# Feature-wise matrix products: three matmuls of 256 columns into the same PSUM columns in place of one of 512 and one of 256 with an addition

## The chip, the core and the metric

The kernel is one program on one core of a Trainium2 chip. The metric is the time of one execution on the device, in microseconds (us). The kernel before was timed in three runs: 2785.09, 2785.18 and 2785.83 us, median 2785.18. One more execution was recorded by the profiler; the rows below come from that one.

## The reference, cut to what matters

The program computes two transformer blocks on 256 tokens of width 2048, in float32. The first block is a sliding-window attention and a gated feed-forward network (`D_FF` 5632). The second is a hybrid mixer (gated linear attention and a pooled branch), a cross-attention to a memory of 256 tokens, and a feed-forward network with a short convolution. Most of the work is products of a normalised activation with a weight matrix:

```python
def swiglu(h, w_gate, w_up, w_down):
    return (silu(h @ w_gate) * (h @ w_up)) @ w_down

def conv_glu_ffn(h, w_up, conv_w, conv_b, w_down):
    u = h @ w_up
    u = conv(u) + conv_b            # along the tokens, one filter for each feature
    gate, val = u[..., :D_FF_2], u[..., D_FF_2:]
    return (silu(gate) * val) @ w_down

q = (h @ w_cq); k = mem_n @ w_ckv[:, :2048]    # cross-attention, queries and keys
```

## The kernel before, in words

**Units.** The function `weight_units` (lines 55 to 99) lists 920 units. A unit is one slice of a weight matrix, 256 rows by 512 columns (512 KB). All engines go through the units in this order, each with its own program. SyncE loads the slice into one of five buffers `raw` (line 376). ScalarE rounds it to float32r, `whi` (line 857), VectorE takes the remainder, `wlo = raw - whi` (line 1273); both have four buffers. The activations lie in SBUF transposed and split in the same way, as `XA`, `XB` or `XC`: `X[w.x][:, k, 0, :]` is the high part of 128 features by 256 tokens and `X[w.x][:, k, 1, :]` the low part. A product of two split numbers is made of three terms, high by high, low by high and high by low; low by low is left out.

**Two kinds of units.** In a row-wise unit (`rows_unit`, lines 426 to 436) the activation is the stationary operand (the weights of the array, 128 columns) and the weight slice is the moving one: lines 433, 434 and 435, 512 columns each, 12 matmuls in a unit. In a feature-wise unit (`feature_unit`, lines 438 to 447) the weight slice is stationary and the activation moves, so the output has the features in the partitions. The change is there. It serves the first projections of both feed-forward networks (`ffn`, lines 67 to 72, 16 feature-wise units for each 512 features), the queries and keys of the linear attention (lines 80 and 81) and of the cross-attention (lines 91 to 94). That is 432 of the 920 units, and 8 pairs of matmuls in each. Line 445 multiplies the high weights with high and low activations side by side, 512 columns, so a PSUM bank holds high-by-high in columns 0 to 255 and high-by-low in columns 256 to 511. Line 446 adds low-by-high, 256 columns, to the first half. Each matmul has a weight load of its own.

**Eviction.** Eight feature-wise units sum up four banks of 128 features each. Then ScalarE copies the second half of a bank to SBUF (`tile_copy` line 968, `qk_copy` line 1037, `cross_copy` line 1107), one bank in each of the next four units. VectorE adds the first half to the copy (`tile_sum` line 1477, `qk_sum` line 1553, `cross_sum` line 1665) and multiplies the sum with a broadcast row of the inverse norms (lines 1482, 1557, 1671). The rest of a feed-forward tile (convolution, silu, product, split into `XB`) follows in later units.

**What sets the order.** Each engine's program is written out by hand as a loop over `u`, with tables (`TILES`, `QK`, `CQK` and others) that say at which `u` a piece of side work stands. TensorE waits before a unit for its split weights (`s.lo`, line 842), for its activation (`operand`) and, at the first unit of a bank group, for the banks' readers (`banks_clear`, lines 712 to 795): for a feature-wise bank on `s.fsum`, `s.gs` or `s.cs`, raised by the addition. ScalarE and VectorE split the weights three units ahead of TensorE (`split_until`, line 345).

Of the kernel before, what the change touches and what calls it, by code (L numbers as in the profile page):

```python
# [11 lines left out]
ACT = mybir.ActivationFunctionType  # L12
AX = mybir.AxisListType

P = 128
# [86 lines left out]
UNITS = weight_units()  # L102
# [73 lines left out]
class Region:  # L176
# [21 lines left out]
    act dve ones xtr xhi xlo sq rms rrt rs dg wd wide res  # L198
    table sine rope mask kv ksq kms krt krope ktr kT
    qe qsq qms qrt qrs qrope qtr qT sco mx exp pn ptr pT pv bxh bx  # L200
    fc fsum fu fw fv silu fm hh hx fzero
    wah wal gn am aT gz lt ln ls pe pm pc pw pxh px cum bT
    gqc gs gqk ge gexp gx gp gsel gB gv sr go gsq gms grt og ogt ogh ogx sg m1 mg mT mxh mx2
    cc cs ckq csc cmx cexp cpn cpt cpT vm cpv oxh ox
    fsq fy fms frt frs yd ya"""


# [3 lines left out]
def build(nc, d):  # L211
# [75 lines left out]
    gX = B.take("gX", [P, 4, 256])  # L287
    gA = B.take("gA", [P, 2, 4, P])
    gB = B.take("gB", [P, 4, P])
    gt = B.take("gt", [P, 4, 256])  # L290
    M.new()
    gv = M.take("gv", [P, 2, 1024])
    sr = M.take("sr", [P, 2, 1024])
# [21 lines left out]
    vm = M.take("vm", [P, 2, D])  # L315
    cp = [M.take(f"cp{i}", [P, 2, 256]) for i in range(2)]
    cpT = [M.take(f"cpT{i}", [P, 2, 256]) for i in range(2)]
    ct = M.take("ct", [P, 4, 256])
    csm = M.take("csm", [P, 32])

    space["A"].new()
# [95 lines left out]
    def tensor():  # L417
# [20 lines left out]
        def feature_unit(u, w):  # L438
            i = u % NSPL
            for j in range(2):  # L440
                both = X[w.x][:, w.xk + j, :, :]
                high = X[w.x][:, w.xk + j, 0, :]
                for f in range(4):
                    b, c = w.banks[f], slice(f * P, (f + 1) * P)
                    pe.matmul(ps[:, b, :], whi[:, i, j, c], both, start=w.begin and j == 0, stop=False)  # L445
                    end = pe.matmul(ps[:, b, 0:256], wlo[:, i, j, c], high, start=False, stop=w.end and j == 1)  # L446
            end.then_inc(s.unit, 1)

        def feed(n, c, bank):
# [199 lines left out]
        def cross_scores(h):  # L649
            pe.wait_ge(s.ckq, 4 * (4 + h) + 4)  # L650
            if h == 0:
                pe.wait_ge(s.cs, 28)
            else:
                pe.wait_ge(s.cexp, h)
            for t in range(2):
                for j in range(4):
                    e = pe.matmul(ps[:, 2, t * 256:(t + 1) * 256], qcT[:, 4 * h + j, t * P:(t + 1) * P],  # L657
                                  kmT[:, 4 * h + j, :], start=j == 0, stop=j == 3)
            e.then_inc(s.csc, 1)
# [7 lines left out]
        def cross_values(h):  # L667
            pe.wait_ge(s.vm, h + 1)
            pe.wait_ge(s.cpT, h + 1)
            if h == 0:  # L670
                pe.wait_ge(s.cs, 32)
            else:
                pe.wait_ge(s.ox, 2 * h)
            for j in range(4):
                for m in range(2):
                    e = pe.matmul(ps[:, j // 2, (j % 2) * 256:(j % 2) * 256 + 256],  # L676
                                  vm[:, m, h * 512 + j * P:h * 512 + (j + 1) * P], cpT[h % 2][:, m, :],
                                  start=m == 0, stop=m == 1)
                if j % 2 == 1:
                    e.then_inc(s.cpv, 1)  # L680
# [31 lines left out]
        def banks_clear(u, w):  # L712
# [13 lines left out]
                    pe.wait_ge(s.res, 2)  # L726
            elif w.weight in ("ffn_w_down", "w_down_2"):
                e, ch = u // U_F2, (w.k // 16) * 4 + (2 if w.k >= 32 else 3)
                pe.wait_ge(s.fsum, tile(e, ch, w.acc // 2, 1 + 2 * (w.acc % 2)) + 1)
            elif U_F1 <= u < U_IN or U_F2 <= u:  # L730
                e = u // U_F2
                base = (U_F1, U_F2)[e]
# [2 lines left out]
                if ch == 0 and which == 0:  # L735
                    pe.wait_ge(s.res, 3 if e == 0 else 23)
                    pe.wait_ge(s.xlo, 2 * FEED_AT[(1, 5)[e], 2] + 2)
                elif ch == 0:
                    pe.wait_ge(s.res, 4 if e == 0 else 24)
                    pe.wait_ge(s.xlo, 2 * FEED_AT[(1, 5)[e], 3] + 2)  # L740
                    pe.wait_ge(s.wide, 1 if e == 0 else 5)
                elif ch % 4 == 0:
                    pe.wait_ge(s.res, (0, 20)[e] + ch + 2 + 2 * which)
                else:
                    pe.wait_ge(s.fsum, tile(e, ch - 1, which, 3) + 1)
            elif u == U_IN:
                pe.wait_ge(s.res, 15)
            elif u == U_IN + 8:
# [4 lines left out]
                pe.wait_ge(s.pe, 2)  # L753
                pe.wait_ge(s.bT, 2)
            elif u in (U_IN + 32, U_IN + 40):
                pe.wait_ge(s.gs, 2 if u == U_IN + 32 else 6)
            elif u in (U_IN + 48, U_IN + 56):
                pe.wait_ge(s.gv, 1 if u == U_IN + 48 else 2)
            elif U_IN + 64 <= u < U_OUT:
# [14 lines left out]
            elif U_CK <= u < U_CV:  # L774
                j = (u - U_CK) // 8
                if j < 2:
                    pe.wait_ge(s.res, 19 + j)
                    pe.wait_ge(s.xlo, 2 * FEED_AT[4, 2 + j] + 2)
                    if j:
                        pe.wait_ge(s.wide, 4)  # L780
                else:
                    pe.wait_ge(s.cs, 4 * (j - 1))
            elif U_CV <= u < U_CO:
                n = (u - U_CV) // 8
                if n < 2:
                    pe.wait_ge(s.cs, 26 + 4 * n)
                else:
                    pe.wait_ge(s.vm, n - 1)
            elif w.weight == "w_co_2":
                if w.acc < 2:  # L790
                    pe.wait_ge(s.vm, 3 + w.acc)
                elif w.acc == 2:
                    pe.wait_ge(s.cpT, 4)
                else:
                    pe.wait_ge(s.ox, 8)
# [54 lines left out]
    def scalar():  # L850
# [110 lines left out]

        def tile_copy(u, e, ch, which, f):
            w = UNITS[u - 1 - f]
            if f == 0:
                act.wait_ge(s.unit, u)
            act.activation(ft[e][which][:, f, :], ps[:, w.banks[f], 256:512], ACT.Copy).then_inc(s.fc, 1)

        def tile_conv(e, ch, which, f):  # L970
            n = which * NF + ch * 4 + f
            act.wait_ge(s.fu, tile(e, ch, which, f) + 1)
# [57 lines left out]
                act.wait_ge(s.cum, b + 1)  # L1030
                act.copy(bT[:, 2 * b:2 * b + 2, :], ps[:, 2 + b, :].rearrange("p (h t) -> p h t", t=256)).then_inc(s.bT, 1)

        def qk_copy(u, i):
            f = i % 4
            if f == 0:
                act.wait_ge(s.unit, u)
            act.activation(gt[:, f, :], ps[:, UNITS[u - 1 - f].banks[f], 256:512], ACT.Copy,
                           scale=1.0 if i >= 4 else float(128 ** -0.5)).then_inc(s.gqc, 1)

        def level_exp(n):  # L1040
            act.wait_ge(s.ge, n)
            act.activation(gE[:, :, :], gE[:, :, :], ACT.Exp).then_inc(s.gexp, 1)
# [56 lines left out]
                e.then_inc(s.mxh, 1)  # L1099

        def cross_copy(u, i):
            f = i % 4
            if f == 0:
                act.wait_ge(s.unit, u)
            act.activation(ct[:, f, :], ps[:, UNITS[u - 1 - f].banks[f], 256:512], ACT.Copy).then_inc(s.cc, 1)

        def cross_exp(h):
            scale = 512 ** -0.5  # L1110
# [47 lines left out]
        for u in range(U_END + 1):  # L1158
# [33 lines left out]
                query_root(q_root_at[u])  # L1192
            if u in ATTEND:
                exponents(ATTEND[u])
            if u in TILES:
                tile_copy(u, *TILES[u])
            if u in tiles1:
                e, ch, which, f = tiles1[u]
                if e == 1:
# [22 lines left out]
                pool_map(POOL2[u])  # L1222
            if u == MI + 22:
                decays()
            if u in QK:
                qk_copy(u, QK[u])
            if u in level_exp_at and level_exp_at[u] < 8:
                level_exp(level_exp_at[u] + 1)
            if u == MI + 55:
# [16 lines left out]
            if u in CQK:  # L1246
                cross_copy(u, CQK[u])
            if u in CSC:
                cross_exp(CSC[u])
            if u in c_turn_at:  # L1250
# [16 lines left out]
    def vector():  # L1267
# [204 lines left out]

        def tile_sum(u, e, ch, which, f):
            n = tile(e, ch, which, f)
            t, off = ft[e][which][:, f, :], 2 * e
            dve.wait_ge(s.fc, n + 1)
            dve.scalar_tensor_tensor(out=t, in0=ps[:, UNITS[u - 1 - f].banks[f], 0:256], scalar=1.0, in1=t,
                                     op0=ALU.mult, op1=ALU.add).then_inc(s.fsum, 1)
            dve.wait_ge(s.fsum, n + 1)
            if f == 0 and ch == 0:  # L1480
                dve.wait_ge(s.wide, (1, 5)[e])
            dve.tensor_tensor(fu[e][which][:, f, off:off + 256], t, wideX[:, :], ALU.mult).then_inc(s.fu, 1)

        def tile_conv(e, ch, which, f):
            n, t = tile(0, ch, which, f), ft[e][which][:, f, :]
# [63 lines left out]

        def qk_sum(u, i):  # L1550
            f = i % 4
            dve.wait_ge(s.gqc, i + 1)
            dve.scalar_tensor_tensor(out=gt[:, f, :], in0=ps[:, UNITS[u - 1 - f].banks[f], 0:256],
                                     scalar=1.0 if i >= 4 else float(128 ** -0.5), in1=gt[:, f, :],
                                     op0=ALU.mult, op1=ALU.add).then_inc(s.gs, 1)
            dve.wait_ge(s.gs, i + 1)
            dve.tensor_tensor((gk if i >= 4 else gq)[:, f, :], gt[:, f, :], wideX[:, :], ALU.mult).then_inc(s.gqk, 1)

        def level_select(n):
            L = STEPS[n]  # L1560
# [100 lines left out]

        def cross_sum(u, i):
            f, n = i % 4, i // 4 % 4
            dve.wait_ge(s.cc, i + 1)
            dve.scalar_tensor_tensor(out=ct[:, f, :], in0=ps[:, UNITS[u - 1 - f].banks[f], 0:256], scalar=1.0,
                                     in1=ct[:, f, :], op0=ALU.mult, op1=ALU.add).then_inc(s.cs, 1)
            dve.wait_ge(s.cs, i + 1)
# [3 lines left out]
            dve.tensor_tensor(o[:, 4 * n + f, :], ct[:, f, :], wide[:, :], ALU.mult).then_inc(s.ckq, 1)  # L1671

        def cross_max(h):
            mx = csm[:, h * 4:h * 4 + 2]
# [212 lines left out]
```

## Time and profile before

| | |
|---|---|
| Median of three runs | 2785.18 us |
| The profiled execution, its own time | 2785.57 us |
| Its span, first to last instruction | 2784.3 us |
| TensorE matmuls, busy | 2734.6 us, 98% |
| TensorE weight loads, busy (under the matmuls) | 2297.5 us, 83% |
| VectorE busy | 1686.0 us, 61% |
| ScalarE busy | 1372.0 us, 49% |
| DMA | 495.5 MB, mean 178 GB/s |
| Mean granted TensorE clock | 0.993 of full speed |

Busy time is the union of the times in which an engine had at least one instruction in flight. Matmuls are pipelined: a matmul begins before the one in front of it has left the array, so the listed duration of one is longer than the time for which it holds the engine. How often they start tells that. Idle time is listed with what ended it.

### The profile page before, as it was taken

How to read it: one execution, taken by the hardware profiler on the slowest of the kernel's cores; microseconds unless marked ns; L12 is line 12 of the kernel's file. 1: busy time of each engine (PE TensorE's matmuls, PEld its weight loads, DVE VectorE, ACT ScalarE, POOL GpSimd, SP SyncE). 2: the span in 40 equal slices, each digit the busy share in tenths (PEclk: the TensorE clock that was granted, in tenths of full speed). 3: DMA queues.
4: the chain of work that ended last, by engine and by line, in shares of the span. 5: the costliest groups of instructions: out<-in, count | busy, mean ns of one | idle time of the engine just before them, and what ended most of it. 6: DMA issues, size and time to landing. Idle time of an engine off the chain costs nothing.

```text
span 2784.3 us, 34701 instructions
## 1 busy us (share of the span) xinstructions
PE 2734.6 (98%) x13940; PEld 2297.5 (83%) x13940; DVE 1686.0 (61%) x2438; ACT 1372.0 (49%) x2040; POOL 0.2 (0%) x4
## 2 busy tenths in 40 slices
PE   8989999999999998999999999999999999999998
PEld 7667888888888886888888888888888888888886
DVE  6666566556655664474555655544568756775676
ACT  6665544444434454445444544444455544553554
POOL 0000000000000000000000000000000000000000
PEclk9999999999999999999999999999999999999999
DMA  6324666666666666768696555554566566656654
GB/s 224 114 91 129 183 186 189 191 188 184 186 197 182 189 179 163 161 157 173 190 190 195 203 183 182 188 161 143 181 181 198 188 198 178 195 179 204 183 188 144
DMA packets 256994, 495.54 MB, mean 178 GB/s; under 512 B 17201, under 2 KB 18481, under 8 KB 256322
## 3 DMA queue, kind: packets, MB, share of 16 engines
q1 hardware_dynamic: 256834, 493.33, 60.1%
q8 instruction: 110, 1.80, 0.3%
q14 instruction: 50, 0.41, 0.0%
HBM read 491.17 MB, written 2.10 MB: 177 GB/s over the span
## 4 chain that ended last, share of the span: by engine, by line
PE 95%; ACT 2%; DVE 2%; DMA 1%; SPq 0%; issue 0%; ACTq 0%; DVEq 0%
PE ps L445 29%; PE ps L433 15%; PE ps L435 15%; PE ps L434 15%; PE ps L446 15%; PE ps L423 1%; PE ps L512 1%; ACT whi L857 1%; PE ps L615 1%; PE ps L676 1%; PE ps L532 1%; PE ps L657 0%; DMA raw<-in_w_in 0%; ACT sS L946 0%; DVE sS L1459 0%
## 5 line engine op out<-in xcount | busy, mean ns | idle before, releaser
L857 ACT CAST whi<-raw 128x1024 fp32r<-128x1024 f32 x920 | 965.4, 1050 | 1259.3 <-PE ps L435 635.1
L1273 DVE TENSOR_TENSOR wlo<-raw,whi 128x1024 fp32r<-128x1024 f32 x920 | 1121.5, 1221 | 689.8 <-ACT whi L857 688.6
L445 PE MATMUL ps<-XA,whi 128*128 128x512 f32 x1792 | 633.4, 399 | 0.0
L445 PE MATMUL ps<-XC,whi 128*128 128x512 f32 x1664 | 588.4, 399 | 0.0
L446 PE MATMUL ps<-XA,wlo 128*128 128x256 f32 x1792 | 502.9, 281 | 0.0
L446 PE MATMUL ps<-XC,wlo 128*128 128x256 f32 x1664 | 467.3, 281 | 0.0
L445 PEld LDWEIGHTS ps<-XA,whi 128*128 128x128 f32 x1792 | 336.7, 188 | 83.4
L433 PE MATMUL ps<-whi,XB 128*128 128x512 f32 x960 | 377.3, 393 | 0.0
L445 PEld LDWEIGHTS ps<-XC,whi 128*128 128x128 f32 x1664 | 312.7, 188 | 77.7
L435 PE MATMUL ps<-whi,XB 128*128 128x512 f32 x960 | 374.3, 390 | 0.0
L434 PE MATMUL ps<-wlo,XB 128*128 128x512 f32 x960 | 374.2, 390 | 0.0
L446 PEld LDWEIGHTS ps<-XA,wlo 128*128 128x128 f32 x1792 | 338.4, 189 | 0.2
L446 PEld LDWEIGHTS ps<-XC,wlo 128*128 128x128 f32 x1664 | 314.3, 189 | 0.2
L433 PE MATMUL ps<-whi,XA 128*128 128x512 f32 x736 | 294.2, 400 | 0.9 <-DVE wlo L1273 0.9
L435 PE MATMUL ps<-whi,XA 128*128 128x512 f32 x736 | 288.5, 392 | 0.0
L434 PE MATMUL ps<-wlo,XA 128*128 128x512 f32 x736 | 288.4, 392 | 0.0
L433 PEld LDWEIGHTS ps<-whi,XB 128*128 128x128 f32 x960 | 180.6, 188 | 39.4 <-issue 2.5
L435 PEld LDWEIGHTS ps<-whi,XB 128*128 128x128 f32 x960 | 180.5, 188 | 37.8
L434 PEld LDWEIGHTS ps<-wlo,XB 128*128 128x128 f32 x960 | 180.7, 188 | 36.5
L433 PEld LDWEIGHTS ps<-whi,XA 128*128 128x128 f32 x736 | 139.4, 189 | 33.6 <-issue 5.3
L435 PEld LDWEIGHTS ps<-whi,XA 128*128 128x128 f32 x736 | 139.3, 189 | 30.0
L434 PEld LDWEIGHTS ps<-wlo,XA 128*128 128x128 f32 x736 | 139.5, 190 | 27.7
(225 smaller groups left out, 1899.1 us busy)
## 6 DMA issues: line engine op xcount, KB each, us to landing
raw<-in_w_up SPq DMA_DIRECT2D x176, 512.0 KB, 3.8
raw<-in_w_in SPq DMA_DIRECT2D x128, 512.0 KB, 5.1
raw<-in_ffn_w_gate SPq DMA_DIRECT2D x88, 512.0 KB, 3.8
raw<-in_ffn_w_up SPq DMA_DIRECT2D x88, 512.0 KB, 3.8
raw<-in_ffn_w_down SPq DMA_DIRECT2D x88, 512.0 KB, 3.7
raw<-in_w_down SPq DMA_DIRECT2D x88, 512.0 KB, 3.7
raw<-in_w_ckv SPq DMA_DIRECT2D x64, 512.0 KB, 4.1
raw<-in_attn_w_qkv SPq DMA_DIRECT2D x40, 512.0 KB, 4.0
```

The lines of the kernel that those rows point to most:

```text
L423: t = pe.transpose(ps[:, bank, c0 + i * P:c0 + (i + 1) * P], src, ident)
L433: pe.matmul(o, xh, whi[:, i, j, :], start=w.begin and j == 0, stop=False)
L434: pe.matmul(o, xh, wlo[:, i, j, :], start=False, stop=False)
L435: end = pe.matmul(o, xl, whi[:, i, j, :], start=False, stop=w.end and j == 1)
L445: pe.matmul(ps[:, b, :], whi[:, i, j, c], both, start=w.begin and j == 0, stop=False)
L446: end = pe.matmul(ps[:, b, 0:256], wlo[:, i, j, c], high, start=False, stop=w.end and j == 1)
L512: e = pe.matmul(ps[:, b, m * nk:(m + 1) * nk], qT[c % 2][:, h, qb * P:(qb + 1) * P], kT[:, c, 0:nk], start=False, stop=m == len(heads) - 1)
L532: e = pe.matmul(ps[64 * (h % 2):64 * (h % 2) + 64, 7, (m // 2) * P:(m // 2 + 1) * P], vt[:, kb, c * 64:c * 64 + 64], pT[n % NPT][:, (m * ( ...
L615: e = pe.matmul(o, left[:, h, t * P:(t + 1) * P], r, start=True, stop=True)
L676: e = pe.matmul(ps[:, j // 2, (j % 2) * 256:(j % 2) * 256 + 256], vm[:, m, h * 512 + j * P:h * 512 + (j + 1) * P], cpT[h % 2][:, m, :], st ...
L857: act.copy(whi[:, u % NSPL, :, :], raw[:, u % NRAW, :, :]).then_inc(s.hi, 1)
L1273: dve.tensor_tensor(wlo[:, u % NSPL, :, :], raw[:, u % NRAW, :, :], whi[:, u % NSPL, :, :].bitcast(F), ALU.subtract).then_inc(s.lo, 1)
```

## The change

A feature-wise product is now three matmuls of 256 columns into columns 0 to 255 of its bank: high weights by high activations, high weights by low activations, low weights by high activations. The second half of the bank is not used. The copies on ScalarE and the additions on VectorE are gone with their buffers `gt` and `ct`; the product with the broadcast row reads PSUM directly (for the linear attention's queries and keys, with the scale in the same instruction). VectorE waits for the unit itself (`s.unit`) at the first of four tiles. TensorE's waits for cleared banks go to the semaphores of those products (`s.fu`, `s.gqk`, `s.ckq`) with the same counts. The diff shows the feed-forward tiles; the linear attention's and the cross-attention's copies, sums and waits change in the same way.

```diff
@@ feature_unit
             for j in range(2):
-                both = X[w.x][:, w.xk + j, :, :]
-                high = X[w.x][:, w.xk + j, 0, :]
+                high, low = X[w.x][:, w.xk + j, 0, :], X[w.x][:, w.xk + j, 1, :]
                 for f in range(4):
-                    b, c = w.banks[f], slice(f * P, (f + 1) * P)
-                    pe.matmul(ps[:, b, :], whi[:, i, j, c], both, start=w.begin and j == 0, stop=False)
-                    end = pe.matmul(ps[:, b, 0:256], wlo[:, i, j, c], high, start=False, stop=w.end and j == 1)
+                    o, c = ps[:, w.banks[f], 0:256], slice(f * P, (f + 1) * P)
+                    pe.matmul(o, whi[:, i, j, c], high, start=w.begin and j == 0, stop=False)
+                    pe.matmul(o, whi[:, i, j, c], low, start=False, stop=False)
+                    end = pe.matmul(o, wlo[:, i, j, c], high, start=False, stop=w.end and j == 1)
             end.then_inc(s.unit, 1)
@@ banks_clear
-                pe.wait_ge(s.fsum, tile(e, ch, w.acc // 2, 1 + 2 * (w.acc % 2)) + 1)
+                pe.wait_ge(s.fu, tile(e, ch, w.acc // 2, 1 + 2 * (w.acc % 2)) + 1)
...
-                    pe.wait_ge(s.fsum, tile(e, ch - 1, which, 3) + 1)
+                    pe.wait_ge(s.fu, tile(e, ch - 1, which, 3) + 1)
@@ scalar
-        def tile_copy(u, e, ch, which, f):
-            w = UNITS[u - 1 - f]
-            if f == 0:
-                act.wait_ge(s.unit, u)
-            act.activation(ft[e][which][:, f, :], ps[:, w.banks[f], 256:512], ACT.Copy).then_inc(s.fc, 1)
@@ vector
         def tile_sum(u, e, ch, which, f):
             n = tile(e, ch, which, f)
-            t, off = ft[e][which][:, f, :], 2 * e
-            dve.wait_ge(s.fc, n + 1)
-            dve.scalar_tensor_tensor(out=t, in0=ps[:, UNITS[u - 1 - f].banks[f], 0:256], scalar=1.0, in1=t,
-                                     op0=ALU.mult, op1=ALU.add).then_inc(s.fsum, 1)
-            dve.wait_ge(s.fsum, n + 1)
-            if f == 0 and ch == 0:
+            off = 2 * e
+            if f == 0:
+                dve.wait_ge(s.unit, u)
                 dve.wait_ge(s.wide, (1, 5)[e])
-            dve.tensor_tensor(fu[e][which][:, f, off:off + 256], t, wideX[:, :], ALU.mult).then_inc(s.fu, 1)
+            dve.tensor_tensor(fu[e][which][:, f, off:off + 256], ps[:, UNITS[u - 1 - f].banks[f], 0:256], wideX[:, :],
+                              ALU.mult).then_inc(s.fu, 1)
```

## Rows read from the trace of the kernel before

**Rows 1.** The page, busy us (share of the span) and instructions of each engine.

```profile
PE 2734.6 (98%) x13940; PEld 2297.5 (83%) x13940; DVE 1686.0 (61%) x2438; ACT 1372.0 (49%) x2040; POOL 0.2 (0%) x4
```

**Rows 2.** Waits of TensorE's matmuls, longest first: total us, times, longest.

```profile
PE ps L532 <- DVE XB L1467: 15.1, 10, 4.1
PE ps L544 <- DVE wal L1514: 9.9, 1, 9.9
...
PE ps L676 <- ACT vm L1125: 0.5, 1, 0.5
```

**Rows 3.** The chain of waits on the page: shares by engine, and by line.

```profile
PE 95%; ACT 2%; DVE 2%; DMA 1%; SPq 0%; issue 0%; ACTq 0%; DVEq 0%
PE ps L445 29%; PE ps L433 15%; PE ps L435 15%; PE ps L434 15%; PE ps L446 15%; PE ps L423 1%; PE ps L512 1%; ACT whi L857 1%; PE ps L615 1%; PE ps L676 1%; PE ps L532 1%; PE ps L657 0%; DMA raw<-in_w_in 0%; ACT sS L946 0%; DVE sS L1459 0%
```

**Rows 4.** Groups of instructions, line 445: count | busy us, mean ns | idle us.

```profile
L445 PE MATMUL ps<-XA,whi 128*128 128x512 f32 x1792 | 633.4, 399 | 0.0
L445 PE MATMUL ps<-XC,whi 128*128 128x512 f32 x1664 | 588.4, 399 | 0.0
```

**Rows 5.** Line 445, 565 to 755 us: ns min/median/max, first and last start.

```profile
L445 PE MATMUL ps<-XA,whi x504: 389/398/404, 577.2 to 754.9; 128*128 128x512 f32 x168
```

**Rows 6.** Line 433, 757 to 846 us, same columns.

```profile
L433 PE MATMUL ps<-whi,XB x128: 389/389/403, 758.1 to 844.5; 128*128 128x512 f32 x128
```

**Rows 7.** Stretches: us, PE busy (count), granted clock, DMA share, GB/s.

```profile
1073.00:1076.00 3.00, 3.00 (x11) 0.50 0.66 197
...
577.00:755.00 178.00, 178.00 (x1009) 1.00 0.63 186
758.00:844.00 86.00, 86.00 (x381) 1.00 0.62 191
```

**Rows 8.** Timeline of the narrow gate product (start us, duration us): pairs of 512 and 256.

```profile
1074.45 0.63 PE L544 MATMUL ps<-XA,wah 128*16 128x512 f32 x1
...
1075.09 0.63 PE L544 MATMUL ps<-XA,wah 128*16 128x512 f32 x1
...
1077.17 0.39 PE L544 MATMUL ps<-XA,wah 128*16 128x512 f32 x1
...
1079.61 0.40 PE L544 MATMUL ps<-XA,wah 128*16 128x512 f32 x1
```

**Rows 9.** Timeline of TensorE inside a feature-wise unit.

```profile
600.03 0.28 PE L446 MATMUL ps<-XA,wlo 128*128 128x256 f32 x1
600.14 0.40 PE L445 MATMUL ps<-XA,whi 128*128 128x512 f32 x1
600.39 0.28 PE L446 MATMUL ps<-XA,wlo 128*128 128x256 f32 x1
```

**Rows 10.** Timeline where a feature-wise unit begins, behind a row-wise one.

```profile
845.19 0.39 PE L445 MATMUL ps<-XA,whi 128*128 128x512 f32 x1
845.41 0.28 PE L446 MATMUL ps<-XA,wlo 128*128 128x256 f32 x1
```

**Rows 11.** Timeline of the weight loads: the one beside the last of rows 9.

```profile
600.39 0.19 PEld L445 LDWEIGHTS ps<-XA,whi 128*128 128x128 f32 x1
```

**Rows 12.** Timeline of one level of the linear attention, weight loads.

```profile
1198.14 1.75 PEld L615 LDWEIGHTS ps<-gX 128*128 128x128 f32 x15
...
1199.81 0.19 PEld L433 LDWEIGHTS ps<-whi,XA 128*128 128x128 f32 x1
```

**Rows 13.** Timeline of the first cross-attention scores; two matmuls further on.

```profile
1836.77 3.61 PE L657 MATMUL ps<-kmT,qcT 128*128 128x256 f32 x16
...
1840.45 0.40 PE L434 MATMUL ps<-wlo,XC 128*128 128x512 f32 x1
```

**Rows 14.** Groups: the feed-forward tiles' copy on ScalarE and addition on VectorE.

```profile
L968 ACT ACTIVATE ft<-ps 128x256 f32<-128x256 f32 x176 | 66.1, 375 | 0.0
...
L1477 DVE SCALAR_TENSOR_TENSOR ft<-ps,ft 128x256 f32<-128x256 f32 x176 | 74.3, 422 | 131.5 <-ACT ft L968 131.1
```

**Rows 15.** Groups: weight loads of line 434.

```profile
L434 PEld LDWEIGHTS ps<-wlo,XB 128*128 128x128 f32 x960 | 180.7, 188 | 36.5
```

More of the change, by code:

```diff
@@ L200 @@
     qe qsq qms qrt qrs qrope qtr qT sco mx exp pn ptr pT pv bxh bx
-    fc fsum fu fw fv silu fm hh hx fzero
+    fu fw fv silu fm hh hx fzero
     wah wal gn am aT gz lt ln ls pe pm pc pw pxh px cum bT
-    gqc gs gqk ge gexp gx gp gsel gB gv sr go gsq gms grt og ogt ogh ogx sg m1 mg mT mxh mx2
-    cc cs ckq csc cmx cexp cpn cpt cpT vm cpv oxh ox
+    gqk ge gexp gx gp gsel gB gv sr go gsq gms grt og ogt ogh ogx sg m1 mg mT mxh mx2
+    ckq csc cmx cexp cpn cpt cpT vm cpv oxh ox
     fsq fy fms frt frs yd ya"""
@@ L289, in build @@
     gB = B.take("gB", [P, 4, P])
-    gt = B.take("gt", [P, 4, 256])
     M.new()
@@ L317, in build @@
     cpT = [M.take(f"cpT{i}", [P, 2, 256]) for i in range(2)]
-    ct = M.take("ct", [P, 4, 256])
     csm = M.take("csm", [P, 32])
@@ L651, in cross_scores @@
             if h == 0:
-                pe.wait_ge(s.cs, 28)
+                pe.wait_ge(s.ckq, 28)
             else:
@@ L670, in cross_values @@
             if h == 0:
-                pe.wait_ge(s.cs, 32)
+                pe.wait_ge(s.ckq, 32)
             else:
@@ L755, in banks_clear @@
             elif u in (U_IN + 32, U_IN + 40):
-                pe.wait_ge(s.gs, 2 if u == U_IN + 32 else 6)
+                pe.wait_ge(s.gqk, 2 if u == U_IN + 32 else 6)
             elif u in (U_IN + 48, U_IN + 56):
@@ L781, in banks_clear @@
                 else:
-                    pe.wait_ge(s.cs, 4 * (j - 1))
+                    pe.wait_ge(s.ckq, 4 * (j - 1))
             elif U_CV <= u < U_CO:
@@ L785, in banks_clear @@
                 if n < 2:
-                    pe.wait_ge(s.cs, 26 + 4 * n)
+                    pe.wait_ge(s.ckq, 26 + 4 * n)
                 else:
@@ L1031, in decays @@
                 act.copy(bT[:, 2 * b:2 * b + 2, :], ps[:, 2 + b, :].rearrange("p (h t) -> p h t", t=256)).then_inc(s.bT, 1)
[L1033 to L1038, printed above, removed]
         def level_exp(n):
@@ L1099, in merge_turn @@
                 e.then_inc(s.mxh, 1)
[L1103 to L1107, printed above, removed]
         def cross_exp(h):
@@ L1194, in scalar @@
                 exponents(ATTEND[u])
-            if u in TILES:
-                tile_copy(u, *TILES[u])
             if u in tiles1:
@@ L1224, in scalar @@
                 decays()
-            if u in QK:
-                qk_copy(u, QK[u])
             if u in level_exp_at and level_exp_at[u] < 8:
@@ L1245, in scalar @@
                 merge_turn(merge_at[u])
-            if u in CQK:
-                cross_copy(u, CQK[u])
             if u in CSC:
@@ L1551, in qk_sum @@
             f = i % 4
[L1552 to L1557, printed above, removed]
+            if f == 0:
+                dve.wait_ge(s.unit, u)
+            dve.scalar_tensor_tensor(out=(gk if i >= 4 else gq)[:, f, :], in0=ps[:, UNITS[u - 1 - f].banks[f], 0:256],
+                                     scalar=1.0 if i >= 4 else float(128 ** -0.5), in1=wideX[:, :],
+                                     op0=ALU.mult, op1=ALU.mult).then_inc(s.gqk, 1)
         def level_select(n):
@@ L1663, in cross_sum @@
             f, n = i % 4, i // 4 % 4
[L1664 to L1667, printed above, removed]
+            if f == 0:
+                dve.wait_ge(s.unit, u)
             if i in (0, 16):
@@ L1670, in cross_sum @@
             o, wide = (qcT, wideX) if i >= 16 else (kmT, wideM)
-            dve.tensor_tensor(o[:, 4 * n + f, :], ct[:, f, :], wide[:, :], ALU.mult).then_inc(s.ckq, 1)
+            dve.tensor_tensor(o[:, 4 * n + f, :], ps[:, UNITS[u - 1 - f].banks[f], 0:256], wide[:, :],
+                              ALU.mult).then_inc(s.ckq, 1)
         def cross_max(h):
```

## The prediction

> **What bounds the kernel now.** I read the busy shares first: TensorE is busy 2734.6 of 2784.3 us, VectorE 61% and ScalarE 49% [rows 1]. The list of waits on TensorE's queue comes second. It runs from the attention values and the narrow gate product down to the memory values, 38 us in all, and names no eviction of a feature-wise product [rows 2]. The chain of waits says the same: TensorE holds 95% of it, and line 445 with line 446 holds 44% [rows 3]. So time can come or go almost only through the pace at which TensorE takes its matmuls.
>
> The durations in the grouped lines are latencies that overlap (399 ns for a matmul of line 445 [rows 4]), and adding them up would count the same time twice. What counts is the distance from start to start. In a stretch of feature-wise units alone, 504 matmuls of line 445 start between 577.2 and 754.9 us [rows 5]: 177.7 / 503 = **353.3 ns per pair**. The row-wise units in 758.1 to 844.5 us hold 128 of line 433, each followed by two more of 512 columns [rows 6]: 86.4 / 127 / 3 = **226.8 ns per matmul of 512**. The granted clock is 1.00 in both stretches, and 0.50 where the narrow gate product begins [rows 7]; those are the levels 2.4 and 1.2 GHz. At the low one a pair takes 0.64 us (1074.45 to 1075.09 [rows 8]), which is 768 columns / 1.2 GHz = 640 ns. So a column takes one cycle, 512 columns are 213.3 ns at full clock and 256 are 106.7 ns. The rest is a cost per matmul: 226.8 - 213.3 = **13.5 ns** in the row-wise units, and 353.3 - 320.0 = 33.3 ns for the two matmuls of a pair.
>
> **The change, part by part.** TensorE: 1792 + 1664 = 3456 pairs [rows 4] become 3456 triples. The columns streamed stay 768 for each. One matmul and one weight load are added for each, 3456 of both, and each triple pays three boundaries between matmuls where the pair paid two. Nothing in the trace shows a 256-column matmul behind another of this kind, so its period is bounded from the rows around it:
>
> (a) Behind 512 columns, a start of line 446 is followed by the next start after 0.11 to 0.12 us, and that one by the next after 0.23 to 0.25 [rows 9]. Taken at its face, a 256-column matmul holds the engine about 117 ns. Three would be 351 ns, 2.3 ns under the pair.
>
> (b) But the 512-column matmul behind a 256 is the slow one. The first of line 445 in its unit, which follows 512 columns, takes 0.22 us to the next start [rows 10], like any in the row-wise units; one behind a 256 takes 353.3 - 117 = 236 ns, 9.5 ns more than 226.8. What a 256 leaves unpaid is charged to its successor. 353.3 - 226.8 = 126.5 ns is what a 256 adds to a stream of 512s, and three of them would be 379.5 ns.
>
> (c) Part of that surcharge belongs to the weight load. The narrow gate product runs the same 512 and 256 columns, with 16-column weights. From 1077.17 to 1079.61 us there are seven pairs [rows 8]: 348.6 ns each, 28.6 over the columns, 14.3 per boundary and so nearly the 13.5 of the row-wise units whatever the length. Full-width weights cost 353.3 - 348.6 = 4.7 ns more per pair. The load for the next matmul starts with the running one and lasts 0.19 us [rows 11]; a 512 covers that, a 256 does not. In the triple every load runs under a 256.
>
> (d) The floor is the load cadence. In a gated-linear-attention level, 16 matmuls of 64 columns have 128-column loads, and 15 of these take 1199.81 - 1198.14 us, 111.3 ns each [rows 12]. Three are 334 ns.
>
> (e) Float32 operands show a smaller boundary: sixteen 256-column matmuls at two cycles a column take (1840.45 - 1836.77 us - 0.227) / 16 = 215.8 ns [rows 13], only 2.5 over their 213.3.
>
> I take the middle term by the nearest rows, a full-width boundary of 13.5 plus 4.7 for a load that a 256 doesn't cover: 3 x (106.7 + 13.5 + 4.7) = **374.7 ns**, 21.4 over the pair, and 3456 x 21.4 ns = **+74 us**. The ends are 334 ns (d) and 379.5 ns (b), or -67 and +91 us.
>
> The Trainium skill, in TensorE: Matmul & The Clock Gate, section Back-to-back issue gap, gives N / 2.4 + 2.5 ns from start to start at full clock. By that rule pair and triple differ by one boundary of 2.5 ns, +9 us in all. For a pair it makes 325 ns where this trace has 353.3, so the trace does not agree with it here.
>
> ScalarE loses 176 + 32 + 8 copies of about 375 ns, some 81 us of work. VectorE loses as many additions of about 423 ns, some 91 us; its product with the broadcast row now reads PSUM [rows 14]. I cost all of this at nothing. VectorE's waits in front of those additions, 131 us of them before the 176 [rows 14], are on the copies and lie under TensorE's stream. Banks come free one copy and one addition earlier, but TensorE shows no wait for them [rows 2]. If that cover were gone, a product of some 420 ns would be exposed once per block of eight units, 54 times, 23 us. But between the fourth tile's product and its bank's next use lie five units, 14 us. VectorE's new wait stands at the first of each four tiles, for the unit that ScalarE awaited before; queued behind it are the split of the next weights, whose lead is three units (8 us). The semaphores that moved (to the product, from the sum) are raised at about the same place in VectorE's order. SyncE's queue is untouched, and transfers only spread with the slower pace. No other wait of [rows 2] is released by a copy or an addition.
>
> Sum against the profiled execution, 2785.57 us (the median of the runs shown is 2785.18, the same within 0.02%): 2785.6 + 74 = **2859.6 us**.
>
> **The rivals.**
> 1. *A boundary costs the same 13.5 ns, whatever load it covers.* For it: 16-column loads cost nearly as much per boundary as 128-column ones. Against it: the 4.7 ns of (c). 3 x 120.2 = 360.6 ns, +25 us, **2811 us**. With the surcharge paid once per triple it is 365.3 ns, 2827 us.
> 2. *The surcharge is all of (b)*, each 256 costing 126.5: 379.5 ns, +91 us, **2876 us**. For it: the 0.22 us of [rows 10] against the 236 ns of (b). I hold this and my forecast to be one mechanism with two sizes.
> 3. *The other side: uniform short matmuls flow at the pace seen behind a 256*, 117 ns or down to the load cadence. 351 ns gives -8 us, **2778 us**; 334 ns gives 2719 us. It decides from 353.3 / 3 = 117.8 ns downward. For it: sixteen loads in a row keep 111.3 ns [rows 12], and (a) is what the starts say. Against it: it has to make the 9.5 ns that line 445 loses behind a 256 a matter of 512-column matmuls alone.
> 4. *One more boundary costs next to nothing*, the 2.5 ns of (e): +8.6 us, **2794 us**. Against it: float32 rows run at two cycles a column, and the two streams at one cycle both show 13.5 or more. The rule of the Trainium skill quoted above comes to the same time.
> 5. *No change to be seen*, or a load that is dropped since two neighbouring matmuls share their weights. In the row-wise units line 434 has the weights of line 433 in front of it and still loads them each of its 960 times [rows 15], so I expect all 3 x 3456 loads.
>
> **How the numbers follow.** Forecast with rival 2, one mechanism: 0.50. Rival 1: 0.22. Rival 4: 0.06. Rival 3: 0.17. No change: 0.05. A measurement of this kernel tells about 0.2% (6 us) from no change. Slower: 0.50 + 0.22 + 0.06 = 0.78. Same: 0.05. Faster: 0.17. The range goes from 2776 us, the mild form of rival 3, to 2888 us, rival 2 with about 1 ns more per matmul. It leaves out the load-bound form of rival 3.
>
> **What would show it.** Right: the three new lines with 3456 matmuls and 3456 loads each; start to start about 125 ns, eight triples taking 3.0 us; durations of the 256-column matmuls near 289 ns in place of 281; row-wise units still at 226.8; granted clock 1.00; the copies gone from ScalarE and VectorE with longer waits of both for TensorE; the span up by 3456 times what the triple gained. Wrong: a period at or under 117.8 ns; a stretch of the row-wise units that moves; a new wait of TensorE on VectorE at lines 724 to 760.

## The result, and the profile after

The changed kernel takes **2807.38 us** (median of four runs, 2805.72 to 2808.44) against 2785.44 us before in the same comparison; the ratio is 1.0078, 95% interval 1.0061 to 1.0096. It is slower by 22 us, where 74 us were forecast: the direction of the forecast held, its size was over three times what came. The profiled execution took 2807.37 us, with a span of 2806.0 us, 21.7 us above the one before.

The page's first part after the change, busy time and instructions of each engine, answers to [rows 1]:

```profile
PE 2758.2 (98%) x17396; PEld 2483.3 (88%) x17396; DVE 1603.7 (57%) x2222; ACT 1315.2 (47%) x1824; POOL 0.2 (0%) x4
```

There are 3456 more matmuls and as many more weight loads (17396 against 13940): none is dropped where two neighbours share their weights. VectorE and ScalarE have 216 instructions less each, 82 and 57 us of busy time, and the span shows no gain from it.

The three new lines in the groups of instructions (count | busy us, mean ns of one | idle us), and the first of them in the stretch of feature-wise units from 565 to 757 us (ns min/median/max, first and last start), which answers to [rows 5]:

```profile
L442 PE MATMUL ps<-XA,whi 128*128 128x256 f32 x1792 | 507.6, 283 | 0.0
L444 PE MATMUL ps<-XA,wlo 128*128 128x256 f32 x1792 | 507.1, 283 | 0.0
L443 PE MATMUL ps<-XA,whi 128*128 128x256 f32 x1792 | 507.1, 283 | 0.0
```

```profile
L442 PE MATMUL ps<-XA,whi x491: 277/283/283, 580.6 to 757.0; 128*128 128x256 f32 x164
```

491 starts in 580.6 to 757.0 us are 176.4 / 490 = **360.0 ns per triple**, where the pair took 353.3. The granted clock is 1.00 from 577 to 755 us, as before, and the middle duration is 283 ns, where the prediction had 289. The timeline of TensorE, the same place as [rows 9]:

```profile
600.03 0.28 PE L442 MATMUL ps<-XA,whi 128*128 128x256 f32 x1
600.15 0.28 PE L443 MATMUL ps<-XA,whi 128*128 128x256 f32 x1
600.27 0.28 PE L444 MATMUL ps<-XA,wlo 128*128 128x256 f32 x1
600.39 0.28 PE L442 MATMUL ps<-XA,whi 128*128 128x256 f32 x1
```

Every start is 0.12 us behind the one before, with no unevenness: 120.0 ns for 106.7 ns of columns. The sum closes: 3456 x (360.0 - 353.3) = +23 us in the feature-wise units. The row-wise units did not move: 113 starts of line 431 (the former 433) from 769.7 to 845.9 us are 226.8 ns per matmul again, as in [rows 6]. The remaining -1.5 us lie in TensorE's waits. The list of them, longest first, answers to [rows 2]:

```profile
PE ps L530 <- DVE XB L1440: 14.9, 9, 4.1
PE ps L542 <- DVE wal L1485: 8.2, 1, 8.2
```

The narrow gate product waits 1.7 us less, and no bank's reader is in the list. The evictions now wait for TensorE itself, 22.4 us on VectorE, and no wait of TensorE is for them:

```profile
L1452 DVE TENSOR_TENSOR fu<-ps,wideX 128x256 f32<-128x256 f32 x176 | 73.8, 420 | 22.4 <-PE ps L444 22.4
```

So the time came from where it was expected, TensorE's pace in the feature-wise units. What has to be explained is 120.0 ns in place of 124.9, and then why the pair costs 353 and not 226.7 + 120.0 = 346.7 ns.

### The profile page after: what moved, and what is told of

Same layout as the page of the kernel before. It is cut to its first block, busy times and chain, and to the rows that moved or that the text cites. A ratio compares the mean times of both kernels' runs of the same rounds, so it can differ in the third digit from the quotient of the medians.

```text
span 2806.0 us, 41221 instructions
## 1 busy us (share of the span) xinstructions
PE 2758.2 (98%) x17396; PEld 2483.3 (88%) x17396; DVE 1603.7 (57%) x2222; ACT 1315.2 (47%) x1824; POOL 0.2 (0%) x4
## 4 chain that ended last, share of the span: by engine, by line
PE 95%; ACT 2%; DVE 2%; DMA 1%; SPq 0%; issue 0%; ACTq 0%; DVEq 0%
PE ps L431 15%; PE ps L433 15%; PE ps L432 15%; PE ps L442 15%; PE ps L444 15%; PE ps L443 15%; PE ps L421 1%; PE ps L510 1%; ACT whi L855 1%; PE ps L613 1%; PE ps L674 1%; PE ps L655 0%; PE ps L530 0%; DMA raw<-in_w_in 0%; ACT sS L944 0%
## 5 line engine op out<-in xcount | busy, mean ns | idle before, releaser
L442 PE MATMUL ps<-XA,whi 128*128 128x256 f32 x1792 | 507.6, 283 | 0.0
L443 PE MATMUL ps<-XA,whi 128*128 128x256 f32 x1792 | 507.1, 283 | 0.0
L442 PE MATMUL ps<-XC,whi 128*128 128x256 f32 x1664 | 471.2, 283 | 0.0
L443 PE MATMUL ps<-XC,whi 128*128 128x256 f32 x1664 | 470.9, 283 | 0.0
L443 PEld LDWEIGHTS ps<-XA,whi 128*128 128x128 f32 x1792 | 344.0, 192 | 0.2
L442 PEld LDWEIGHTS ps<-XA,whi 128*128 128x128 f32 x1792 | 344.0, 192 | 0.2
L443 PEld LDWEIGHTS ps<-XC,whi 128*128 128x128 f32 x1664 | 319.4, 192 | 0.2
L442 PEld LDWEIGHTS ps<-XC,whi 128*128 128x128 f32 x1664 | 319.4, 192 | 0.2
```

Source lines behind the costliest of these rows:

```text
L442: pe.matmul(o, whi[:, i, j, c], high, start=w.begin and j == 0, stop=False)
L443: pe.matmul(o, whi[:, i, j, c], low, start=False, stop=False)
```

## The experiments

My theory once the result was known: a matmul that takes one cycle a column costs 13.3 ns beside its columns whatever its length, and the pair pays extra because it alternates lengths. The rivals were that the 120 ns is made by the weight loads, by the shared PSUM columns, or by the changed eviction.

**1. Three matmuls with the old eviction** (`halves`)

```diff
...
-                    pe.matmul(ps[:, b, :], whi[:, i, j, c], both, start=w.begin and j == 0, stop=False)
+                    pe.matmul(ps[:, b, 0:256], whi[:, i, j, c], high, start=w.begin and j == 0, stop=False)
+                    pe.matmul(ps[:, b, 256:512], whi[:, i, j, c], low, start=False, stop=False)
```

> The kernel before with its eviction kept; only the 512-column matmul is cut in two, high weights by high activations into columns 0 to 255 and high weights by low activations into columns 256 to 511 of the bank. Theory (each matmul of one cycle a column costs 13.3 ns beside its columns, wherever it writes): 120.0 ns from start to start for each, 360 ns a triple, time 2807 us like the changed kernel, so the smaller eviction was worth nothing. Rival (the 120 ns of the changed kernel come from three matmuls that add into the same columns): the matmul that goes to the other half takes less, at or under the 117 ns seen behind 512 columns, a triple 351 ns and the time near 2778 us. Rival (the smaller eviction hid a loss): slower than 2807 us by more than 6 us.

2807.7 us, ratio 1.0079 (1.0064 to 1.0094). The same stretch, the matmul that goes to the other half:

```profile
L445 PE MATMUL ps<-XA,whi x491: 282/283/283, 580.5 to 756.9; 128*128 128x256 f32 x164
```

Again 360.0 ns per triple. The whole loss is the cut of the 512-column matmul. Adding into the same columns costs nothing, and the copies and additions that the change removes were worth nothing.

**2. and 3. The same pairs in another order** (`g_four`, `g_unit`)

```diff
             for j in range(2):
                 both = X[w.x][:, w.xk + j, :, :]
+                for f in range(4):
+                    b, c = w.banks[f], slice(f * P, (f + 1) * P)
+                    pe.matmul(ps[:, b, :], whi[:, i, j, c], both, start=w.begin and j == 0, stop=False)
+            for j in range(2):
                 high = X[w.x][:, w.xk + j, 0, :]
                 for f in range(4):
                     b, c = w.banks[f], slice(f * P, (f + 1) * P)
-                    pe.matmul(ps[:, b, :], whi[:, i, j, c], both, start=w.begin and j == 0, stop=False)
                     end = pe.matmul(ps[:, b, 0:256], wlo[:, i, j, c], high, start=False, stop=w.end and j == 1)
```

This is `g_unit`; `g_four` has one loop over j, with both loops over f inside it.

> The kernel before with another order of the same matmuls: for each j the four of 512 columns first, then the four of 256. Theory (a pair costs 353.1 instead of 226.7 + 120.0 = 346.7 ns since lengths alternate, and each change from 256 to 512 costs the 6.4 ns once): eight pairs take 8 x 346.7 + 2 x 6.4 = 2786 ns, 38 ns under the 2825 of before, times 432 units = -17 us, 2769 us. Rival (the 6.4 ns belong to each matmul of 512 columns that reads the high and the low activations side by side): eight pairs still 2825 ns, 2785 us. Rival (256-column matmuls into different banks cost other than 120 ns): seen in their start-to-start time inside the group of four.

> As the previous kernel, but the eight matmuls of 512 columns of a unit first, then its eight of 256. Theory: one change of length in a unit, 8 x 346.7 + 6.4 = 2780 ns, 45 ns under before, times 432 = -19 us, 2766 us; a version faster than both kernels. Rival (no cost of alternation): 2785 us. Rival (the low weights' matmuls come later, whi and wlo buffers are freed later and TensorE waits for the split of the next weights): no gain, with waits of line 433 or 445 for VectorE's split in the profile.

`g_four` took 2777.18 us (ratio 0.9972, 0.9960 to 0.9983), `g_unit` 2772.30 us (0.9953, 0.9938 to 0.9967). Both beat the kernel before (2785.18 us in this comparison) by more than their intervals, with the same matmuls in another order. Each fell some 6 to 8 us short of the number expected. The timeline of `g_unit`, TensorE, one unit and the next one's beginning, where the view is cut off (start us, duration us of the run of equal instructions):

```profile
605.43 2.00 PE L444 MATMUL ps<-XA,whi 128*128 128x512 f32 x8
607.28 1.12 PE L449 MATMUL ps<-XA,wlo 128*128 128x256 f32 x8
608.23 0.63 PE L444 MATMUL ps<-XA,whi 128*128 128x512 f32 x2
```

The eight of 256 take 0.95 us, 119 ns each. The eight of 512 take 1.85 us, 231 ns each and not 226.7. Start to start, averaged by position over the 64 units between 565 and 757 us, the matmuls of 512 behind a 256 read 233, 236, 228, 232 and 231 ns before they settle at 226.7, 27 ns more in all; the first 256 behind a 512 takes 113 ns and gives 7 back. A change of length is thus not a single 6.4 ns, as both expectations had it. It unsettles the next five matmuls of 512 and costs about 20 ns net. In `g_four`, with only four of 512 in a row, the same sum over the positions gives 16.5 ns, and in the pair of before it is 353.3 - 346.7 = 6.6 ns. So no single price for each change holds, and both expectations took that of the pair for longer groups: this is what they fell short by (864 x 10 ns = 9 us and 432 x 13 ns = 6 us). In the pair of before the length changes with every matmul and the pace never settles, which is my account of the 353.

**4. Fewer changes still** (`snake`)

```diff
+            if w.k // 2 % 2 == 0:
+                wide()
+                end = short()
+            else:
+                short()
+                end = wide()
```

`wide` is the first loop of `g_unit`, `short` the second.

> As g_unit, but each second feature-wise unit runs its eight matmuls of 256 columns first and its eight of 512 after, so that equal lengths meet at unit borders: 216 changes from 256 to 512 in place of 432. Theory (each change from 256 to 512 is followed by five or six matmuls of 512 that take 228 to 236 ns in place of 226.7, 27 ns in all, and the first 256 behind a 512 gives 7 back, 20 ns net per change): 216 x 20 = 4.3 us under g_unit, 2768 us. Rival (what g_unit won came from the order of the banks or from fewer steps between high and low weights, not from the number of changes): 2772 us or above. Rival (an odd unit needs its low weights at its start): TensorE waits for VectorE's split, visible in its waits, and the time is above g_unit's.

**2767.57 us** (five runs, 2767.21 to 2768.10), ratio 0.9936 (0.9922 to 0.9949). The timeline across two units, cut off at 607 us:

```profile
600.72 3.82 PE L445 MATMUL ps<-XA,whi 128*128 128x512 f32 x16
604.38 2.08 PE L454 MATMUL ps<-XA,wlo 128*128 128x256 f32 x16
606.29 1.09 PE L445 MATMUL ps<-XA,whi 128*128 128x512 f32 x4
```

Sixteen of 512 now take 3.66 us, 229 ns each. Halving the number of changes gave the 4.3 us expected of it (4.7 measured), so the gain follows the count of length changes. The steps between high and low weights are halved along with them here, but the changed kernel makes such steps in every triple, at one length, and each start there comes 120.0 ns behind the last. Nor is it the order of banks: `g_unit` and `snake` change the bank with every matmul, and both lengths settle, at 226.7 and 120.0 ns. This is the fastest version of the study that computes the whole result: 18 us under the kernel before, 40 us under the changed one.

**5. Shorter pieces in two weights** (`pieces`)

```diff
+                cuts = {"ffn_w_gate": (0, 128, 256), "ffn_w_up": (0, 192, 256)}.get(w.weight, (0, 256))
...
+                    for n, (p, q) in enumerate(zip(cuts, cuts[1:])):
+                        pe.matmul(o[:, p:q], whi[:, i, j, c], high[:, p:q], start=w.begin and j == 0 and n == 0, stop=False)
...
```

The other two terms get the same loop over pieces.

> The changed kernel with the matmuls of 256 columns cut further in one place each: ffn_w_gate into 128 + 128 columns, ffn_w_up into 192 + 64; all other weights stay at 256. Theory (period is the larger of columns / 2.4 GHz + 13.3 ns and the load cadence of 111.3 ns seen in the linear attention): 111.3 ns for 128, for 192 and for 64 columns; 6 x 111.3 = 668 ns per former triple of 360, 704 triples in each of the two, +434 us, 3241 us. Rival (120.0 ns is itself the cadence of float32r weight loads and not 106.7 + 13.3): all of them 120 ns, 720 ns per triple, +507 us, 3314 us. Rival (no floor by the loads here): 66.7 ns for 128 columns, 400 ns per triple, some 2835 us in the first half of it alone.

3242.82 us in one run; 3241 was expected by the theory. The timeline where the pieces have 128 columns:

```profile
599.80 0.28 PE L444 MATMUL ps<-XA,whi 128*128 128x128 f32 x1
...
600.92 0.27 PE L445 MATMUL ps<-XA,whi 128*128 128x128 f32 x1
```

Ten matmuls in 1.12 us, 112 ns each. Where the pieces have 192 and 64 columns, six starts take 669 ns on the average of the trace, 111.6 ns each, but unevenly: single starts are from 51 to 173 ns apart, so the 111 ns bind on the average and not from each start to the next. The floor set by full-width loads is thus where the linear attention showed it [rows 12], and 120 ns lies above it: the loads' cadence alone doesn't make the 120.

**6. Row-wise units cut in two** (`rows256`)

```diff
-                    pe.matmul(o, xh, whi[:, i, j, :], start=w.begin and j == 0, stop=False)
+                    for h in (slice(0, 256), slice(256, 512)):
+                        pe.matmul(o[:, h], xh, whi[:, i, j, h], start=w.begin and j == 0 and h.start == 0, stop=False)
```

The other two lines are cut in the same way.

> The kernel before with every matmul of 512 columns of the row-wise units cut into two of 256 (three terms for columns 0 to 255, then three for 256 to 511); the feature-wise units stay pairs. Theory (a matmul costs 13.3 ns beside its columns in any unit): 120.0 ns each in the row-wise units, 488 x 12 = 5856 more matmuls x 13.3 ns = +78 us, 2863 us. Rival (the price is one of the feature-wise units, where weights are the stationary operand and change every matmul): less than 120 ns in the row-wise units. Rival (2.5 ns per added matmul, as float32 rows show): +15 us, 2800 us.

2850.48 us, ratio 1.0232 (1.0218 to 1.0246). Line 434 here (the high weights in the row-wise units), 760 to 860 us:

```profile
L434 PE MATMUL ps<-whi,XB x250: 281/284/284, 770.1 to 859.8; 128*128 128x256 f32 x125
```

89.7 / 249 / 3 = 120.1 ns: the price of a short matmul is the same where the activation is the stationary operand. The total was +65 us where +78 was expected. Summed from start to start over the trace, the row-wise units gained 74 us, and the side work between units gave 10 back. Of these, 5.9 us are the wait in the narrow gate product, 4.0 in place of 9.9 us, at which TensorE arrives later; the rest I did not trace.

**7. Other lengths with full-width loads** (`lengths`; the other output columns of these products are left out)

```diff
+                    n = {"ffn_w_down": 384, "w_down_2": 320, "w_co_2": 192, "w_out_2": 448}.get(w.weight, 512)
-                    o = ps[:, w.banks[t], :]
+                    o = ps[:, w.banks[t], 0:n]
...
```

The moving operands are cut to `0:n` as well. The time, 2616.91 us in one run, is no test, as the expectation says.

> The kernel before with shorter matmuls in four of its row-wise weights, full-width loads throughout (the remaining output columns are left out): w_out_2 448 columns, ffn_w_down 384, w_down_2 320, w_co_2 192. Theory A (the cost beside the columns is a share of them, 17/16 of columns / 2.4 GHz): 198.3, 170.0, 141.7 ns from start to start, and 111.3 ns (the load cadence) for 192. Theory B (13.3 ns for each matmul of any length): 200.0, 173.3, 146.7 and 111.3 ns. Under A the 6.7 ns that a 256 of full width has over 113.3 is a price of short matmuls, and should appear at some length on the way down; under B there is nothing more to explain with full-width loads. The time is no test here, since the units get so short that the transfers and the splits can become the bound.

For 384 columns, line 434 from 733 to 800 us; for the others, a first and a last row of a run in the timeline, 18 matmuls apart for 320, 8 for 448 and 27 for 192:

```profile
L434 PE MATMUL ps<-whi,XB x128: 334/334/343, 733.8 to 799.9; 128*128 128x384 f32 x128
```

```profile
2379.77 0.31 PE L434 MATMUL ps<-whi,XB 128*128 128x320 f32 x1
...
2382.41 0.31 PE L434 MATMUL ps<-whi,XB 128*128 128x320 f32 x1
```

```profile
1499.86 0.36 PE L434 MATMUL ps<-whi,XB 128*128 128x448 f32 x1
...
1501.48 0.36 PE L436 MATMUL ps<-whi,XB 128*128 128x448 f32 x1
```

```profile
1879.79 0.27 PE L434 MATMUL ps<-whi,XA 128*128 128x192 f32 x1
...
1882.81 0.27 PE L434 MATMUL ps<-whi,XA 128*128 128x192 f32 x1
```

| columns | columns / 2.4 GHz | start to start | beside the columns |
|---|---|---|---|
| 512 | 213.3 ns | 226.8 ns | 13.5 |
| 448 | 186.7 | 1.62 us / 8 = 202.5 | 15.8 |
| 384 | 160.0 | 66.1 us / 127 / 3 = 173.5 | 13.5 |
| 320 | 133.3 | 2.64 us / 18 = 146.7 | 13.4 |
| 256 | 106.7 | 120.0 | 13.3 |
| 192 | 80.0 | 3.02 us / 27 = 111.9 | the floor by the loads |

From 256 columns upward and with full-width loads the cost is per matmul and not a share of the columns; a proportional 17/16 would have given 170 ns for 384 and 142 for 320. Only 448 has 2.4 ns more, which I can't explain.

**8. to 12. Narrower and flatter weights** (`narrow_three`, `width96`, `tall64`; `narrow_pair`, `width16`; the rest of the features, or of the sums, is left out)

```diff
-                    o, c = ps[:, w.banks[f], 0:256], slice(f * P, (f + 1) * P)
+                    o, c = ps[0:64, w.banks[f], 0:256], slice(f * P, f * P + 64)
```

This is `narrow_three`, on the changed kernel; `width96` has 96 for 64; `tall64` takes rows 0 to 63 of weights and activations and all columns; `narrow_pair` and `width16` make the same cut, 64 and 16 columns, in the pair of the kernel before.

> The changed kernel with only 64 of each 128 weight columns loaded in the feature-wise units (half of the features is left out), so each weight load is shorter and all else is the same. Theory (13.3 ns are paid per matmul of one cycle a column, not for the load): 120.0 ns from start to start, 2807 us. Rival (the load of 128 columns that a 256 does not cover sets the 120 ns): less than 120 ns, down to 109 ns (106.7 + 2.5), a triple 327 to 350 ns and 2693 to 2772 us.

> The changed kernel with 96 of each 128 weight columns in the feature-wise units (a quarter of the features is left out). With 64 columns a 256-column matmul took 113.4 ns, with 128 it takes 120.0. Theory (a load that is no longer than the stream above it costs nothing; the load of 128 columns, 106.7 ns at 1.2 GHz and 111.3 in cadence, is too near the 113.3 ns): 113.3 ns with 96 columns, 340 ns per triple, 2738 us. Rival (each weight column costs the stream the same share, 6.7 ns for 64 columns more): 116.7 ns, 350 ns per triple, 2773 us.

> The changed kernel with only 64 of 128 rows (partitions) of weights and activations in the feature-wise units, all 128 weight columns (half of each sum is left out). Theory (the 6.7 ns come from the number of weight columns to load, which stays 128): 120.0 ns and 2807 us. Rival (they come from the volume read from SBUF, which is halved as with 64 columns): 113.3 ns, 2738 us.

> The kernel before with only 64 of each 128 weight columns loaded in the feature-wise units (half of the features is left out). Theory (the 6.4 ns of a pair are the price of alternating lengths): a pair stays at 353 ns, 2785 us. Rival (the step of the prediction: 4.7 ns of it belong to a full-width load that a 256 does not cover): 348.6 ns as in the narrow gate product, or 349 to 351 for half the width, 2769 to 2778 us.

> The kernel before, pairs of 512 and 256, with 16 of each 128 weight columns in the feature-wise units (seven eighths of the features are left out): the widths of the narrow gate product, from which the prediction took its 13.5 ns per boundary and its 4.7 ns for a wide load. Theory (a pair with narrow loads costs 17/16 of its columns as with 64 columns; the gate product's 348.6 ns was its own, in a burst of some ten pairs behind a stop): 340 ns per pair, 2740 us. Rival (16-column loads do cost 348.6 ns per pair): 2770 us.

Line 442 of the first three in the same stretch, one row from each kernel in this order:

```profile
L442 PE MATMUL ps<-XA,whi x512: 276/276/281, 570.0 to 743.8; 128*64 128x256 f32 x171
```

```profile
L442 PE MATMUL ps<-XA,whi x512: 274/278/282, 575.0 to 752.8; 128*96 128x256 f32 x171
```

```profile
L442 PE MATMUL ps<-XA,whi x489: 275/280/382, 581.1 to 756.8; 64*128 64x256 f32 x163
```

Per matmul these are 173.8 / 511 / 3 = 113.4 ns with 64 weight columns, 116.0 with 96, and 175.7 / 488 / 3 = 120.0 with 128 columns of 64 rows. The times were 2737.96, 2766.64 and 2813.41 us, one run each (the 6 us that the last has over the changed kernel are not in the pace of these matmuls, and I leave them open).

So my theory fell as a statement about all widths: 120 ns is not paid for the matmul alone. The cost beside the columns depends on how many weight columns are loaded (and on the output rows, which narrow with them), and not on the volume that is read. The rival of a share for each column foresaw 116.7 for the width of 96 and was nearer than my 113.3.

In the pair, line 446 of `narrow_pair` and of `width16`, and TensorE's timeline in `narrow_pair`:

```profile
L446 PE MATMUL ps<-XA,wlo x512: 273/274/280, 570.6 to 744.4; 128*64 128x256 f32 x171
```

```profile
L446 PE MATMUL ps<-XA,wlo x512: 274/279/281, 574.0 to 752.9; 128*16 128x256 f32 x171
```

```profile
600.01 0.39 PE L445 MATMUL ps<-XA,whi 128*64 128x512 f32 x1
600.24 0.27 PE L446 MATMUL ps<-XA,wlo 128*64 128x256 f32 x1
600.35 0.39 PE L445 MATMUL ps<-XA,whi 128*64 128x512 f32 x1
```

With 64 columns a pair takes 173.8 / 511 = 340.1 ns, and the time is 2741.26 us. Theory (353) and rival (348.6 to 351) both stood too high. What is more, 340.1 is 226.7 + 113.4, a settled 512 and the 256 of `narrow_three`: alternating lengths shows no price here. Over this trace a 512 behind a 256 takes 227.6 ns to the next start, where it took 236.2 before. The price of changing lengths is thus one of full-width weights too, and not of the change alone (a stream of 512s with 64 weight columns was not run, so 226.7 is carried over from full width).

With 16 columns the pair takes 350 ns in this stretch; the time, 2770.24 us against 2785.87, makes it (15.6 us / 3456) 4.5 ns under the 353.3 of before, 348.8 over the whole program, as the rival said. The narrow gate product's 348.6 [rows 8] was no accident of a short burst, as I had expected, but what 16-column loads cost in a pair. And 64 columns cost less than 16. A narrower load isn't a cheaper one throughout, and two widths don't tell the price of a load.

## Why the prediction was wrong, point by point

- **What bounds the kernel, the reading by starts, the count of matmuls and loads:** as stated. The span moved by TensorE's pace in the 3456 groups and by nothing else of size.
- **Evictions costed at nothing:** shown by `halves`, 2807.7 against 2807.4 us.
- **The step that failed is the middle term of the sum,** 106.7 + 13.5 + 4.7. The 13.5 measured 13.3 in all three matmuls. The 4.7 "for a load that a 256 doesn't cover" measured 0 on top of it: a 256 with a full-width load costs 13.3 ns beside its columns and a 512 costs 13.5. It was 3 x 4.7 x 3456 = 49 us of the 74 forecast, all but a few us of the miss. I got it by comparing two alternating streams, the pair and the gate product, and then multiplied it by three for a stream that doesn't alternate. `width16` nearly repeats the 4.7 in the pair (4.5), so the difference was real there. The width of the weights counts in the uniform stream too (`narrow_three`, 6.6 ns less at 64 columns), but as something to take off below full width, and not to add at full width, where a 256 costs what a 512 does. The direction of the forecast came from the 13.5 for one more boundary, which held.
- **Reading (b)** had the fact and an incomplete owner: the matmul of 512 behind a 256 is late by 9.5 ns, but with full-width loads this comes with the change of length (`g_four`, `g_unit`, `snake`), and a 256 behind a 256 doesn't have it. With 64 weight columns the lateness all but vanishes in the same pairs (`narrow_pair`), so (c) was right that the width of the weights has a part in it. Rival 2, 126.5 ns each, fell with it.
- **Reading (a)** was wrong as the pace of a uniform stream (117 ns), and reading (d), the floor by loads, holds where it binds (`pieces`, `lengths`).
- **Rival 1 has the number, and its reason only for full-width loads:** 3 x 120.2 = 360.6 ns and 2811 us were stated for it, 360.0 ns and 2807 us measured. I gave it 0.22, against 0.50 for the surcharge. The row that I set against it, the 4.7 ns of (c), came from 16-column weights and mixed lengths; the row that spoke for it, the row-wise units, had full-width loads and one length, which is what the change makes. "Whatever load it covers" is not so: in triples a boundary cost 6.7, 9.3 and 13.3 ns with 64, 96 and 128 weight columns. What the prediction gave for this rival, that 16 columns cost nearly as much as 128, held for 16 columns alone: with 64 columns a boundary in a pair costs 10 ns, with 16 it costs 14.4. Had the change narrowed the loads to 64 columns, rival 1 would have missed: 340.1 ns a triple (`narrow_three`) against its 360.6.
- **Rival 3 (faster)** fell at its own point of decision, 117.8 ns, by 2.2 ns. **Rival 4** fell with 13.3 against 2.5 ns per added matmul, in the row-wise units too (`rows256`).
- The prediction's rule from the Trainium skill (TensorE: Matmul & The Clock Gate, section Back-to-back issue gap) gives 109 ns for 256 columns and 216 for 512, estimates by its formula. The section calls that the spacing of the isolated matmul, without a budget for loads. The streams here take 120.0 and 226.8 with a load for each matmul, and the measurement decides. The Trainium skill, same page, section LDWEIGHTS (loading the stationary operand), gives columns / 1.2 GHz for a load, an estimated 106.7 ns for 128 columns; the cadence of 112 ns in `pieces` is 5 ns above it.

## What to carry to other kernels

A float32r matmul with full-width weights cost its columns plus 13.3 ns here (256 columns and more), so cutting one of 512 columns in two costs that much each time. Removing copies from engines that don't bound gave nothing back. With full-width weights, group matmuls of equal length: the order alone took 18 us (0.6%) off a kernel whose tensor engine was 98% busy. When a cost is read from a stream of mixed lengths or of another weight width, don't carry it to a uniform stream; take the row that is alike in both.

## What the runs showed of the hardware that was not expected

- With full-width weights a change from matmuls of 256 to 512 columns unsettles the pace: 233, 236, 228, 232, 231 ns before 226.7, about 20 ns net for each change in groups of eight, 16.5 in groups of four, 6.6 in pairs. Undoing half of 432 changes gave 4.7 us. With 64 weight columns the pairs show no such price (340.1 ns).
- The cost beside the columns of a 256-column matmul depends on the number of weight columns: 6.7 ns at 64, 9.3 at 96, 13.3 at 128, and not on the rows (120.0 ns with 64 of them). In pairs with one of 512 columns it was 20 ns for both at 64 columns, 29 at 16 and 33 at 128.
- Why 13.3 ns are paid at all, why the order of widths is 64, 96, 128 in triples and 64, 16, 128 in pairs, and why 448 columns cost 2.4 ns more, stays open. No run separated the load of the weights from the width of the output, and float32r matmuls always came with a load of their own here, so one without a load wasn't tried. Float32 matmuls at two cycles a column kept to 2.5 ns [rows 13].
